# A trunk layer on one core: input LayerNorm reordered, small S5 matmuls moved by a block, expert look-ups moved into the up-projection

## What is computed

```python
h = layer_norm(x, ln_in_g, ln_in_b)
z = h @ w_in                                  # q, k, v, ssm_in, two gates
y_attn = chunk_attention(q, k, v, rel_bias)   # 8 heads of 128
y_ssm = gelu(s5_scan(ssm_in, ...)); y_ssm = y_ssm * sigmoid(y_ssm @ w_ssm_glu)
mix = (sigmoid(g_attn) * (y_attn @ w_attn_up) + sigmoid(g_ssm) * (y_ssm @ w_ssm_up)) @ w_out
h = layer_norm(alpha * h + mix, ln1_g, ln1_b)
ple = rms_norm(p @ ple_w_in) * sigmoid(h @ ple_w_gate)
# PEER: 8 heads of queries against 2 x 128 keys, top 16 of each half, top 16 of their 256 sums,
# expert = 128 * first key + second key; gelu(h . u[expert]) times a softmax weight, times v[expert]
h = layer_norm(alpha * h + peer(h) + ple, ln2_g, ln2_b)
```

## Time and profile before

| | |
|---|---|
| runs | 4217.67 us median of 3 (4217.20 to 4218.58) |
| profiled execution | 4217.22 us, span 4215.4 us |
| busy | PE 97%, DVE 51%, ACT 30%, POOL 43% |
| mean granted TensorE clock | 0.987 |

### The profile page before, as it was taken

The page is one execution under the profiler, slowest core; times in us unless marked ns, Lnnn a source line. Parts: engine busy times, 40 slices in busy tenths (PEclk is TensorE's granted clock), DMA queues, the critical chain, the costliest instruction groups (busy, mean ns, idle before and its releaser), DMA issues.

```text
span 4215.4 us, 51809 instructions
## 1 busy us (share of the span) xinstructions
PE 4088.7 (97%) x18480; PEld 3373.0 (80%) x18480; DVE 2145.3 (51%) x2760; ACT 1247.9 (30%) x1497; POOL 1829.0 (43%) x1054
## 2 busy tenths in 40 slices
PE   3999999999999999999999999999999999999997
PEld 3888888878886887788888888888878888888886
DVE  6555555556413569822122222212228777878778
ACT  2233223342223223232323323222223333333322
POOL 6334433434444444378788887000013333342432
PEclk7999999999999999999999999999999999999999
DMA  4444444434431236577777777653347877878775
GB/s 183 136 158 147 148 161 152 147 120 150 169 134 71 94 134 222 182 217 217 214 222 213 221 217 213 222 214 122 130 147 302 321 301 301 316 291 316 308 301 199
DMA packets 325560, 846.22 MB, mean 201 GB/s; under 512 B 98281, under 2 KB 176105, under 8 KB 256265
## 3 DMA queue, kind: packets, MB, share of 16 engines
q1 hardware_dynamic: 146024, 546.93, 36.1%
q10 hardware_dynamic: 101664, 164.19, 11.7%
q0 software_dynamic: 77824, 134.52, 10.7%
HBM read 765.05 MB, written 215.74 MB: 233 GB/s over the span
## 4 chain that ended last, share of the span: by engine, by line
PE 85%; DVE 6%; issue 3%; DVEq 3%; POOLq 1%; DMA 1%; POOL 0%; ACT 0%; ACTq 0%
PE bank L1054 18%; PE bank L1056 18%; PE bank L1055 18%; PE bank L1284 8%; PE bank L1285 8%; PE bank L1286 8%; PE bank L1191 2%; PE bank L1193 2%; PE bank L1192 2%; DVEq L1636 1%; DVE top_i L1554 1%; DVE top_i L1544 1%; DVE res L1299 1%; DVE top_v L1541 0%; PE bank L1098 0%
## 5 line engine op out<-in xcount | busy, mean ns | idle before, releaser
L1054 PE MATMUL bank<-h_hi,whi 128*128 128x512 f32 x3584 | 1407.8, 393 | 23.3 <-POOL wlo L656 20.9
L1056 PE MATMUL bank<-h_hi,wlo 128*128 128x512 f32 x3584 | 1398.2, 390 | 0.0
L1055 PE MATMUL bank<-h_lo,whi 128*128 128x512 f32 x3584 | 1397.6, 390 | 0.0
L656 POOL TENSOR_TENSOR wlo<-raw,whi 128x1024 fp32r<-128x1024 f32 x280 | 711.3, 2562 | 983.0 <-ACT whi L787 491.5
L1299 DVE TENSOR_TENSOR wlo<-raw,whi 128x2048 fp32r<-128x2048 f32 x248 | 568.0, 2290 | 1059.4 <-ACT whi L991 1040.8
L1054 PEld LDWEIGHTS bank<-h_hi,whi 128*128 128x128 f32 x3584 | 675.4, 188 | 163.5 <-POOL wlo L656 21.2
L1056 PEld LDWEIGHTS bank<-h_hi,wlo 128*128 128x128 f32 x3584 | 674.7, 188 | 141.6
L1055 PEld LDWEIGHTS bank<-h_lo,whi 128*128 128x128 f32 x3584 | 675.4, 188 | 138.1
L696 POOL DMA_INDIRECT gates_d<-sel_g,place_u x384 | 665.0, 1732 | 162.0 <-issue 90.1
L1284 PE MATMUL bank<-whi,ew_hi 128*128 128x512 f32 x1536 | 599.3, 390 | 13.8 <-DVE wlo L1299 13.8
L1285 PE MATMUL bank<-wlo,ew_hi 128*128 128x512 f32 x1536 | 598.7, 390 | 0.0
(11 more groups left out here) (270 smaller groups left out, 3353.6 us busy)
## 6 DMA issues: line engine op xcount, KB each, us to landing
raw<-in_weights SPq DMA_DIRECT2D x388, 1024.0 KB, 4.9
v_rows_d<-in_weights ACTq DMA_DIRECT2D x96, 1024.0 KB
v_rows_d<-in_weights SPq DMA_DIRECT2D x32, 1024.0 KB
gates_d<-zeros SPq DMA_DIRECT2D x32, 768.0 KB, 9.8
act_d<-mt ACTq DMA_DIRECT2D x128, 192.0 KB
act_in<-act_d SPq DMA_DIRECT2D x32, 768.0 KB, 7.9
gate_in<-gates_d SPq DMA_DIRECT2D x32, 768.0 KB, 10.7
gate_d<-g_out ACTq DMA_DIRECT2D x32, 256.0 KB, 2.0
```

The source lines that it names most:

```text
L656: pool.tensor_tensor(wlo[slot][:, part], raw[slot][:, part], whi[slot][:, part].bitcast(F32), ALU.subtract).then_inc(lo_made, 1)
L1054: pe.matmul(bank[:, :], whi[slot][:, cols], rhs_hi[:, c, :], start=c == 0, stop=False)
L1055: pe.matmul(bank[:, :], whi[slot][:, cols], rhs_lo[:, c, :], start=False, stop=False)
L1056: last = pe.matmul(bank[:, :], wlo[slot][:, cols], rhs_hi[:, c, :], start=False, stop=c == DC - 1)
```

## The change

1. Input LayerNorm: VectorE computes (x - mean) * g in one pass; ScalarE multiplies by 1/std; b is added only on the turned chunks, from a column per chunk (`b_cols`), by ScalarE as it rounds to `h0_hi` and by VectorE as it subtracts to `h0_lo`. Chunks are turned four tiles to a bank, in seven banks; TensorE turns chunks 7 to 15 between the chunks of block 0.
2. The sine and cosine chain moves from GpSimd to VectorE, ahead of the tiles; `pow_up` moves to VectorE, `lev` to GpSimd. Slab 0's low part comes before the step factors' end.
3. The stored residual lacks b; b is loaded at the output projection and added to `res` there (four more sums).
4. Heads: block 0 of the next head follows the last product of a head. Tables come behind block 2 instead of 1, state inputs behind block 3 instead of 2 (and into `ps_y`). On VectorE the bias and maximum of scores 0 and 1 come before the scan, and the `lev_s` copy just before it.
5. The look-up of the picks leaves the gate projection's loop and becomes a loop of its own behind `picks_made`, over all heads' stored positions; its equality products are 256 wide. `DVE_FROM` is 12.
6. In the tail the last tile's statistics follow the last low part (m == 6 instead of 5).

```diff
-DVE_FROM = 8
+DVE_FROM = 12
+TURN_BANKS = 7
...
             load_x(0)
-            load_x(1)
...
+            for t in range(1, TT):
+                load_x(t)
+            sp.dma_start(b_rows[:, :], vecs[1:2, :].rearrange("a (c p) -> (a c) p", p=P)).then_inc(b_rows_landed, 16)
+            load_slab(0, 0)
             sp.dma_start(b_raw[:, :, :, :], b_in).then_inc(b_landed, 16)
+            load_slab(1, 1)
...
+            for s in range(2):
+                load_slab(AT_OUT + s, s)
+
+            sp.wait_ge(merged, DC + 1)
+            sp.dma_start(b_ln_in[:, :], row(1)).then_inc(ln_in_landed, 16)
...
-            sp.wait_ge(merged, DC + 1)
+            sp.wait_ge(h_ready, TT)
             sp.dma_start(ln_g[:, :], row(2)).then_inc(ln1_landed, 16)
...
+            low_part(0, 0)
+
+            pool.wait_ge(angles_made, 1)
...
+            low_part(0, 1)
             pool.wait_ge(b_landed, 32)
             cmul(pool, bb[:, 0], bb[:, 1], f_wide, [b_raw[:, 0], b_raw[:, 1]], half_t1, half_t2)
...
+            pool.sem_inc(bb_made, 1)
+            low_part(1, 0)
+
+            pool.wait_ge(pow_made, 1)
+            pool.tensor_copy(lev[:, :, :, 0:1], pow_up[:, :, :, LC:LC + 1])
...
+                act.wait_ge(rstd_ready, t + 1)
+                for part in (slice(0, D),) if t < TD else (slice(512 * n, 512 * (n + 1)) for n in range(4)):
+                    act.activation(xt[:, t, part], xt[:, t, part], copy, scale=rstd[:, t:t + 1]).then_inc(x_normed, 1)
...
+            for c in range(DC):
+
+                act.wait_ge(x_turned, c + 1)
+                act.activation(h0_hi[:, c, :], ps[1 + c % TURN_BANKS][:, :], ACT.Identity, bias=b_cols[:, c:c + 1]
+                               ).then_inc(h0_rounded, 1)
+                if c in (5, 9):
+                    first_hi(1, c // 9)
...
+            def first_block():
+                for c in range(DC):
+                    if c % 8 == 0:
+                        pe.wait_ge(lo_made, c // 8 + 4)
+                    cols = slice(c * P, (c + 1) * P)
+                    pe.wait_ge(h0_made, c + 1)
...
+                    if c + TURN_BANKS < DC:
+
+                        for t in range(TT):
+                            turn = turn_x(t, c + TURN_BANKS)
+                        turn.then_inc(x_turned, 1)
...
-                blk(0)
                 blk(1)
+
+                blk(2)
 
                 pe.wait_ge(ef_made, i + 2)
...
-                blk(2)
+                blk(3)
 
                 pe.wait_ge(in_map_made, i + 1)
                 pe.wait_ge(u_landed, 128 * (i + 1))
+                pe.wait_ge(branch_made, 2 * i + 2)
...
-                blk(3)
 
                 pe.wait_ge(qkv_made, 3 * i + 2)
-                pe.wait_ge(h_filled, i + 1)
                 scores(0)
                 scores(1)
                 blk(4)
...
+                if follows:
+                    blk(8)
...
+                stt(xt[:, t, :], xt[:, t, :], mv[:, t, 0:1], g_in[:, :], ALU.subtract, ALU.mult)
+                dve.wait_ge(std_ready, t + 1)
+                dve.drain()
+                dve.reciprocal(rstd[:, t:t + 1], std[:, t:t + 1]).then_inc(rstd_ready, 1)
...
+                stt(h0_lo[:, c, :], ps[1 + c % TURN_BANKS][:, :], b_cols[:, c:c + 1], h0_hi[:, c, :].bitcast(F32), ALU.add,
+                    ALU.subtract).then_inc(h0_made, 1)
...
+                bias_and_max(0)
+                bias_and_max(1)
+
+                dve.wait_ge(lev_made, 1)
+                dve.tensor_copy(lev_s[:, :, :, :], lev[:, :, sl, :])
+                dve.drain()
                 dve.wait_ge(h_filled, i + 1)
                 for k in range(6):
...
             dve.wait_ge(res_landed, 16 * TT)
+            dve.wait_ge(ln_in_landed, 32)
+            for t in range(TT):
+                bias(res, b_ln_in, t)
+            dve.drain()
...
+                dve.tensor_copy(pos[:, :, at], top_i[:, :, :])
+                dve.drain()
+            dve.sem_inc(picks_made, 1)
...
+            with dve.Fori(0, RH) as j:
+                at, one, two = bass.ds(j * TOPK, TOPK), bass.ds(2 * j, 1), bass.ds(2 * j + 1, 1)
+                wide = [P, TT, TOPK, TOPK]
+                for t in range(TT):
+                    for eq, of in ((eq_a, pos_af), (eq_b, pos_bf)):
+                        tt(eq[:, t, :, :], iota[:, 0:TOPK].unsqueeze(1).to_broadcast([P, TOPK, TOPK]),
+                           of[:, t, at].unsqueeze(2).to_broadcast([P, TOPK, TOPK]), ALU.is_equal)
...
-                if m == 5:
+                if m == 6:
                     dve.drain()
                     for c in range(4):
                         quarter(res, TD, c)
```

More of the change, by code:

```diff
@@ L594, in _, with low_part @@
                 pool.drain()
[L596 to L619, removed]
+            def low_part(j, slot):
+                for half in range(2):
+                    part = slice(half * HALF, (half + 1) * HALF)
+                    pool.wait_ge(hi_made, 4 * j + 2 * slot + half + 1)
+                    pool.tensor_tensor(wlo[slot][:, part], raw[slot][:, part],
+                                       whi[slot][:, part].bitcast(F32), ALU.subtract).then_inc(lo_made, 1)
+            low_part(0, 0)
+            pool.wait_ge(angles_made, 1)
             pool.tensor_scalar(R("u"), R("em"), 1.0, None, ALU.add)
@@ L750, in turned_hi @@
                     for g in range(4):
[L751 removed]
+                        act.wait_ge(turned, 16 * (first - 1) + 4 * t + g + 1)
                         act.activation(dst[:, 4 * g:4 * g + 4, t * P:(t + 1) * P],
@@ L816, in s5_out @@
                     act.dma_start(y_d, y_sc[:, :, :]).then_inc(y_stored, 16)
-                step(0)
-                act.wait_ge(prm_ready, 1)
+                if not begins:
+                    split_next(0)
+                wait_block(0)
+                act.wait_ge(bb_made, 1)
                 act.activation(u_cs[:, :, :], ps_p[0][:, :].rearrange("p (c s) -> p s c", s=LC), copy)
@@ L828, in _ @@
                 act.activation(q_h[:, :], ps_p[1][:, :], copy).then_inc(qkv_made, 1)
+                step(2)
+                act.activation(k_h[:, :], ps_p[0][:, :], copy).then_inc(qkv_made, 1)
                 act.wait_ge(e_turned, i + 1)
@@ L1060, in turn @@
             def turn(tiles, first):
-                if not first:
-                    pe.wait_ge(ident_made, 1)
                 for t in range(TT):
@@ L1174, in _ @@
                 last.then_inc(pv_done, 1)
+                if follows:
+                    blk(8)
+            with pe.Fori(0, HEADS - 1) as i:
+                head(i, True)
+            head(HEADS - 1, False)
             def two_blocks(n, slot, blk, rhs, pieces=False):
@@ L1472, in _ @@
                 bias_and_max(1)
+                dve.wait_ge(lev_made, 1)
+                dve.tensor_copy(lev_s[:, :, :, :], lev[:, :, sl, :])
+                dve.drain()
+                dve.wait_ge(h_filled, i + 1)
+                for k in range(6):
+                    n = NC - 2**k
+                    src = h_st[:, :, :, 1:1 + n]
+                    ta, tb = (z[:, 0:512].rearrange("p (r q n) -> p r q n", r=2, q=CB_Q)[:, :, :, 0:n]
+                              for z in (t1, t2))
+                    a_re, a_im = (lev_s[:, ri, :, k:k + 1].unsqueeze(1).to_broadcast([P, 2, CB_Q, n])
+                                  for ri in range(2))
+                    tt(ta, src, a_re, ALU.mult)
+                    tt(tb, src, a_im, ALU.mult)
+                    dve.drain()
+                    tt(ta[:, 0], ta[:, 0], tb[:, 1], ALU.subtract)
+                    tt(ta[:, 1], ta[:, 1], tb[:, 0], ALU.add)
+                    dve.drain()
+                    tt(h_st[:, :, :, 1 + 2**k:], h_st[:, :, :, 1 + 2**k:], ta, ALU.add)
+                    dve.drain()
+                for r in range(2):
+                    rows = slice(ST * r, ST * (r + 1))
+                    dve.memset(h_pair[rows, :, :, 1 - r, :], 0.0)
+                    last = dve.tensor_copy(h_pair[rows, :, :, r, :], h_st[rows, :, :, 0:NC])
+                last.then_inc(scanned, 1)
+                dve.drain()
                 divide(0)
```

259 lines of the change are left out of this document (141 added, 118 removed).

## The result

| | before | after |
|---|---|---|
| median of the runs | 4217.8 us (4 beside those of after) | 4245.66 us (4; 4242.85 to 4246.94) |
| profiled execution | 4217.22 us, span 4215.4 | 4244.56 us, span 4242.6 |
| mean granted TensorE clock | 0.987 | 0.986 |

The ratio after to before is 1.0065, 95% interval 1.0048 to 1.0082: slower by 28 us in the medians and by 27.3 between the profiled executions, where 4242 was forecast.

The account below looks back on a forecast made before the run. Matmuls, 85% of the chain of waits, were taken as the bound, so only TensorE's idle or slow-clock time counts. 4217.2 - 37 (start) - 20.5 (gates) + 80 (heads) + 2.4 (tail) = 4242 us; range 4195 to 4260.

Parts of the forecast that it names:

- Start: Before head 0's first scores: earlier projection matmul and no wait for the tables, first scores near 99.5 instead of 136.8, 37 us saved.
- I add half again: done at 16: Sine and cosine chain on VectorE at the start: 7 us of small steps from 5.4 on, lengthened by half for GpSimd's blocking.
- 30 and 44: Bounds of the start's saving in us: 30 if GpSimd doubles VectorE's chain of small steps, 44 if it does not slow it.
- the start gains little: Rival at the start: GpSimd and VectorE block each other step by step, tables late again, 17 us less won, 4259; chance 0.1.
- Heads: TensorE waits for the scan in each of eight heads: 7.9 us plus 2.1 of slow clock, 10.0 a head, 80 us lost.
- a product and a copy wait for it, 3.5 us more: End of the scan in each head: GpSimd's third low part delays two short VectorE instructions, bringing the scan from 26.0 to 29.5 us.
- a third product waits too: Condition of the heads' upper bound, at GpSimd's third low part: 10.8 us lost a head, 86 us in all.
- Whole-instruction blocking: Rival in the heads' scan: a low part holds the product behind it 2.33 us instead of 2.1; 4252, chance 0.07.
- Gate projection: VectorE's loop without the look-ups takes 15 to 17 us a pass, so TensorE no longer waits; 20.5 us saved.
- Look-ups: Moved to VectorE's idle time in the up-projection: 97 us, 117 with the work around them, hidden with 14 us to spare.
- Output projection: Adding b to the residual there takes VectorE 9.2 us, hidden by two blocks (22 us); no cost.
- Tail: At the end VectorE's last low part no longer hides ScalarE's scaling of the last tile: 2.4 us slower, between 0 and 3.

Follow-up runs that it names:

- experiment 8: Against the kernel of experiment 2: the four sums of b at the output projection only 64 columns wide, the other columns left out; 4154.84 us, one execution.
- experiment 2: Against the changed kernel: the products that need the scan moved behind block 6, ScalarE's copy of their result after the third gate's store; 4158.64 us median, ratio to before 0.9858.
- y_later_tail5: Against the kernel of experiment 2: the last tile's statistics back ahead of the last low part (m == 5); 4155.08 us median, 4155.07 when run once more.

## Why the prediction was right

The sign, the size (4242 against 4244.6 in the profile) and the mechanism hold: TensorE's wait for the scan in each head. By its steps:

- **Start**, 37 forecast, 40.0 measured. The mis-sized term is VectorE's chain of small steps: "I add half again: done at 16". It was done at 11.4. VectorE's timeline of its first and last step:

```profile
4.93 0.72 DVE L1341 TENSOR_TENSOR prm<-prm 128x32 f32<-128x32 f32 x4 [3.54 <-DMA prm<-in_log_dt]
...
11.19 0.18 DVE L1394 TENSOR_SCALAR prm<-prm 128x32 f32<-128x32 f32 x1
```

  29 instructions in 6.4 us, against 7 bare: GpSimd's own small steps did not slow it. The two bounds given for this step, 30 and 44, do not follow from its own numbers: the chain doubled or not slowed moves the sum by 3.5 us either way, so to 33.5 and 40.5. The first projection matmul came at 39.1 instead of 44.5. Block 0 took 17.9 us (17 forecast). What gave 2.3 back is the wait at 83.8 for a low part of GpSimd, which was not foreseen (GpSimd was at `lev`, one of the steps moved to it, until 81.2; from 69 to 78 all but one of its steps of 128x32 took 0.56 to 0.85 us beside VectorE's table products of 512 and 576 columns, against 0.24 to 0.31 before and after that). The rival "the start gains little" fell here.
- **Heads**, 80 forecast, 86.8 measured. The scan was put at 29.5 and took 30.4; the step that was off is "a product and a copy wait for it, 3.5 us more": two products waited, 4.1. The first two low parts cost 8.55 (8.3 forecast). The window was 21.9 us instead of 21.6. Wait 8.6 (7.9), clock 2.3 (2.1): 10.85 a head against 10.0, just past the upper bound of 10.8. That bound was put down to "a third product waits too"; by 2.1 us a product this would be about 12, and what came are two products in full.
- **Whole-instruction blocking.** The six losses are 2.15, 2.15 (half of 4.30), 2.2, 2.05, 2.15 and 1.97 us, 2.1 on average, as the row of before had it, and not 2.33. By the Trainium skill (SBUF - State Buffer, "Who interferes with whom") whoever comes first has the shared ports for its whole instruction, and the other is blocked. The trace agrees: taken one by one, each of the six products ends 0.15 to 0.54 us behind the end of the GpSimd half that it met. It had begun 0.1 to 0.5 us into that half, so it lost the rest of it and not the whole.
- **Gate projection**, 20.5 forecast, 22.9 measured with the shorter wait at the expert values; 13.6 of it between blocks 1 and 15, where 13.7 was forecast.
- **Look-ups**, hidden with 14 us to spare: 13.8. The loop took 92.7 us (97 forecast).
- **Output projection**, nothing forecast, 1.5 measured. Two steps failed. "4 x 2.3 = 9.2 us of VectorE" left out that GpSimd's low parts run beside them: 15.5 us, and the low parts were longer in turn. And "the next slab is due more than a block later" left out that the load of b waits in SyncE's queue ahead of it: ScalarE waited 7.3 us for that slab. Together they made the 1.4 us (experiment 8). The 22 us cover was read for VectorE's first use alone, and not for GpSimd, which is the one that TensorE waited for.
- **Tail**, 2.4 forecast, 2.2 to 2.3 measured, and the gap of 2.24 us ahead of the last tile's gain is the named one.

The errors of start (-3), heads (+7), gates (-2) and output projection (+1.5) partly cancel. That the total is within 3 us, where the heads alone are off by 7, is in part luck.

## What to carry to other kernels

When TensorE's small work is moved by a block, measure the distance from each producer to its consumer before and after: the tables moved and nothing happened, the state inputs moved, their consumer stayed, and the distance fell from 35 us to 24.6, of which the scan has 22. Such a window is to be held against the length of the work as it runs beside the neighbour engine (30 us), not bare (17.7). And a good move and a bad one can come in the same diff: as made, the six parts cost 28 us; with one consumer moved along with its producer, the same six gain 59 (experiment 2). A queue is such a path too: a load that waits for a computation holds up every load behind it.

## What the hardware showed that was not expected

Two profiled executions of the very same kernel (`y_later_tail5` and `y_later_tail5_b`) took 4153.85 and 4159.72 us. The waits of TensorE are the same in both to within 1 us in all; what differs is how long the granted clock stays at 1.2 GHz once a wait is over. The stretch behind the 7.3 us wait before the first block of the expert values, by windows of 1 us (columns: window, its length, TensorE busy, matmuls, granted clock, DMA share, GB/s). The first execution, whose wait ends at 3096.94:

```profile
3099.00:3100.00 1.00, 1.00 (x4) 0.50 1.04 426
3100.00:3101.00 1.00, 1.00 (x5) 0.88 0.92 385
3101.00:3102.00 1.00, 1.00 (x6) 1.00 1.05 442
```

The second, whose wait ends at 3098.44:

```profile
3102.00:3103.00 1.00, 1.00 (x4) 0.50 1.04 442
3103.00:3104.00 1.00, 1.00 (x4) 0.50 1.04 442
3104.00:3105.00 1.00, 1.00 (x4) 0.73 0.97 410
```

About 3.3 us at half clock in the one and 6.1 in the other, so the second, 1.5 us behind as it came to this wait, is 2.8 behind afterwards. The same happens at the last wait before the end: matmuls of 0.63 us stand for 3.1 us in the first execution and for 6.1 in the second, 1.5 us more. After a short wait in between the first keeps its clock (1.64 us of wait) while the second loses it for a time (1.84 us of wait, 0.97 over 50 us). The slow stretch behind that one costs 1.6 us. So between these two executions the clock's cost of one and the same wait differs by up to 1.6 us. In the eight executions of each, the version with a 3.3 us wait near its end scatters more (4153.6 to 4159.7) than the one without (4157.4 to 4159.6), although its median is lower. Why the clock takes longer in one than in the other, no run here shows.

Second, small steps of VectorE and GpSimd side by side (128x32) hardly slowed each other: VectorE's 29 took 6.4 us with GpSimd at 0.25 to 0.35 us a step in the same time. It is a short product of VectorE (0.3 to 0.7 us) behind a long half of GpSimd that multiplies in length, and in the same way a small step of GpSimd beside a wide product of VectorE (0.56 to 0.85 us beside 512 and 576 columns). The row of before from which the prediction feared more, 2.25 us for a step of GpSimd, stood beside a 2048-wide product.
